# Seven products per pair in the second up projection too, its output split inside the down projection, and the weight sums moved

## The reference

```python
def swiglu(h, w_gate, w_up, w_down):
    return (jax.nn.silu(h @ w_gate) * (h @ w_up)) @ w_down
```

## Time and profile before

| | us |
|---|---|
| median of 3 runs (range) | 1692.26 (1689.1 to 1695.09) |
| the profiled execution: its own time, its span | 1692.44, 1690.6 |
| PE busy | 1623.7 (96% of the span) |
| DVE, ACT, POOL busy | 1115.1, 723.6, 344.0 |

### The profile page before, as it was taken

How to read it: one execution, slowest core, us unless ns; L and a number is a source line. 1 busy time by engine, 2 the same in 40 slices (tenths; PEclk the granted TensorE clock), 3 DMA queues, 4 the chain that set the end, 5 groups by cost and what they waited for, 6 DMA issues and landing times.

```text
span 1690.6 us, 23590 instructions
## 1 busy us (share of the span) xinstructions
PE 1623.7 (96%) x9069; PEld 1377.3 (81%) x9069; DVE 1115.1 (66%) x1793; ACT 723.6 (43%) x1158; POOL 344.0 (20%) x835
## 2 busy tenths in 40 slices
PE   6489999999999999999999999999989999999997
PEld 5378888888877877778888888888878899999886
DVE  6988666676664677646333336756746688888877
ACT  5465333332344767745222222234215544444554
POOL 2011877877861100000010110000010000000000
PEclk9789999999999999999999999999999999999999
DMA  8922344455477743455677774458973234555664
GB/s 346 383 86 92 110 151 148 136 181 173 138 163 154 157 125 131 119 137 152 218 183 213 195 196 138 129 171 217 261 207 114 86 118 157 153 158 157 194 190 140
DMA packets 169505, 282.26 MB, mean 167 GB/s; under 512 B 31489, under 2 KB 110705, under 8 KB 166066
## 3 DMA queue, kind: packets, MB, share of 16 engines
q1 hardware_dynamic: 137490, 218.36, 40.6%
q0 software_dynamic: 16992, 55.06, 14.5%
q10 hardware_dynamic: 14912, 7.34, 1.6%
HBM read 262.90 MB, written 70.77 MB: 197 GB/s over the span
## 4 chain that ended last, share of the span: by engine, by line
PE 86%; DVE 5%; DMA 4%; ACT 2%; issue 1%; SPq 1%; POOL 0%; DVEq 0%; ACTq 0%
PE bank L2207 26%; PE bank L2209 26%; PE bank L2208 26%; DVE ada L1419 1%; PE bank L2568 1%; PE bank L2541 1%; PE bank L2386 1%; DMA u_scratch<-us 1%; DVE htok L1403 1%; PE bank L2247 1%; PE bank L2697 1%; DMA raw<-in_fox_out 1%; ACT junk_h L914 1%; DMA raw<-in_fox_in 1%; DMA ada<-in_ada_w 1%
## 5 line engine op out<-in xcount | busy, mean ns | idle before, releaser
L2207 PE MATMUL bank<-hh,w_hi 128*128 128x512 f32 (+1 forms) x1440 | 520.8, 362 | 6.2 <-POOL hl L2202 3.9
L2208 PE MATMUL bank<-hl,w_hi 128*128 128x512 f32 (+1 forms) x1440 | 517.5, 359 | 0.0
L2209 PE MATMUL bank<-hh,w_lo 128*128 128x512 f32 (+1 forms) x1440 | 517.4, 359 | 0.0
L1316 DVE TENSOR_TENSOR w_lo<-raw,w_hi 128x1024 fp32r<-128x1024 f32 x320 | 373.5, 1180 | 196.6 <-ACT w_hi L846 191.5
L846 ACT ACTIVATE w_hi<-raw 128x1024 fp32r<-128x1024 f32 x320 | 325.4, 1021 | 378.1 <-DMA raw<-in_dn 114.7
L2207 PEld LDWEIGHTS bank<-hh,w_hi 128*128 128x128 f32 x1440 | 274.1, 190 | 48.3 <-POOL hl L2202 4.3
L2209 PEld LDWEIGHTS bank<-hh,w_lo 128*128 128x128 f32 x1440 | 274.0, 190 | 40.4
L2208 PEld LDWEIGHTS bank<-hl,w_hi 128*128 128x128 f32 x1440 | 274.0, 190 | 39.0
L2207 PE MATMUL bank<-w_hi,hid 128*128 128x512 f32 x352 | 138.1, 392 | 0.0
L2209 PE MATMUL bank<-w_hi,hid 128*128 128x512 f32 x352 | 137.1, 389 | 0.0
L2208 PE MATMUL bank<-w_lo,hid 128*128 128x512 f32 x352 | 137.0, 389 | 0.0
(11 more groups left out here) (354 smaller groups left out, 2595.0 us busy)
## 6 DMA issues: line engine op xcount, KB each, us to landing
raw<-in_up SPq DMA_DIRECT2D x94, 512.0 KB, 3.6
raw<-in_dn SPq DMA_DIRECT2D x55, 512.0 KB, 4.5
ada<-in_ada_w SPq DMA_DIRECT2D x24, 1024.0 KB, 8.5
v_scratch<-in_up POOLq DMA_DIRECT2D x25, 768.0 KB, 7.5
v_scratch<-in_dn POOLq DMA_DIRECT2D x24, 704.0 KB, 6.6
raw<-in_fox_in SPq DMA_DIRECT2D x32, 512.0 KB, 4.2
raw<-v_scratch SPq DMA_DIRECT2D x61, 256.0 KB, 2.7
raw<-in_up SPq DMA_DIRECT2D x57, 256.0 KB, 2.9
```

The lines of the kernel that those rows point to most:

```text
L1316: dve.tensor_tensor(w_lo[:, n % RING, 0:w], raw[:, n % RING, 0:w], w_hi[:, n % RING, 0:w].bitcast(F32), ALU.subtract).then_inc(lo_done, 1)
L2207: pe.matmul(dst, w_h, r_h, start=first, stop=False, skip_group_check=True)
L2208: pe.matmul(dst, w_h, r_l, start=False, stop=False, skip_group_check=True)
L2209: return pe.matmul(dst, w_l, r_h, start=False, stop=last, skip_group_check=True)
```

## The change

up2 now also does its pairs as seven products, for 18 of 22; `PLAIN2 = 4` stay plain. It needs 36 sums of its own. All sums are one chain now, in the order up2 (36), up3 (42), down3 (32): 16 between the turn tables, 34 over the 39 slots of fox, 28 in up2 from slot 4 on with one for each 2.5 slots, and the last 32 in up3, one for each 2 slots from slot 2 on. A slot of a pair counts like any other, and a pair has four of them now, not two.

up2's output goes unsplit to `hid_raw`. The combinations of `h` lie in the last tiles of `hid`, so only tiles 0 to 9 are split among the pairs, and tiles 10 to 21 in the first six slots of down2.

```diff
+UP2 = Stage("up2", 0, 1, 2, S_UP2, S_PAIRS2, PLAIN2, 0, 0, ((4, 7), (7, 10), (10, 13), (13, 16), (16, 19), (19, 22)))
+UP3 = Stage("up3", 1, 2, 4, S_UP3, S_PAIRS3, PLAIN3, UP2.paired, UP2.sums,
+            ((2, 5), (5, 8), (8, 11), (12, 15), (15, 18), (18, 20), (20, 22)))
+EARLY_HID = 10
...
+            def load_up(st):
+                src, i = dram[st.name], st.index
+                for n in range(2 * st.plain):
+                    load_fm(st.first + n, src[2 * st.tile(n // 2) + n % 2])
...
+                sp.wait_ge(sum_step, 16 * (st.sums_before + st.sums))
+                for p in range(st.paired):
+                    n, j = st.pairs + 4 * p, st.tile(st.plain + p)
+                    gate, val = src[2 * j], src[2 * j + 1]
+                    load_halves(n, gate[:, 0:T], v4[i][j])
+                    load_halves(n + 1, v2[i][j], gate[:, T:D])
+                    load_halves(n + 2, v1[i][j])
+                    load_halves(n + 3, val[:, T:D])
...
-            sp.wait_ge(sum_step, 16 * (UP_SUMS + 32))
-            for i, src in enumerate(sources):
+            for i, (src, sums) in enumerate(zip(sources, (0, 12, 24, 24, 32, 32, 32))):
+                sp.wait_ge(sum_step, 16 * (UP_SUMS + sums))
...
+            def split_hid_hi(j):
+                act.wait_ge(val_done, j + 1)
+                act.activation(hid[:, j, 0, :], hid_raw[:, j, 1, :], ACT.Copy).then_inc(hid_hi, 1)
...
+                    if st is UP2 and p < EARLY_HID:
+                        split_hid_hi(p)
...
+                    if q == 3 and EARLY_HID + 2 * idx < HT:
+                        if idx == 0:
+                            act.wait_ge(slot_mm, first)
+                        split_hid_hi(EARLY_HID + 2 * idx)
+                        split_hid_hi(EARLY_HID + 2 * idx + 1)
...
-            silu_up(S_UP2, 1, BANK_B[2])
+            silu_up_pairs(UP2)
...
+            def split_hid_lo(j):
+                dve.wait_ge(hid_hi, j + 1)
+                dve.tensor_tensor(hid[:, j, 1, :], hid_raw[:, j, 1, :], hid[:, j, 0, :].bitcast(F32), ALU.subtract)\
+                   .then_inc(hid_done, 1)
...
-            sums = up_sums()
+            sums = itertools.chain(up_sums(UP2), up_sums(UP3), down_sums())
             for k in range(PAIRS // 2):
                 turn_tables(k)
                 next(sums)
-            for t in range(UP_SUMS - PAIRS // 2):
-                pool.wait_ge(slot_mm, S_V + 1 + 3 * t // 2)
+            for t in range(34):
+                pool.wait_ge(slot_mm, S_V + 1 + 39 * t // 34)
                 next(sums)
-            assert next(sums, None) is None
-            weight_sums(S_UP2 + 2)
+            for t in range(UP_SUMS - 50):
+                pool.wait_ge(slot_mm, S_UP2 + 4 + 5 * t // 2)
+                next(sums)
             for i in range(KT):
                 pool.wait_ge(yh_done, i + 1)
                 pool.tensor_tensor(hl[:, i, :], yfm[:, i, :], hh[:, i, :].bitcast(F32), ALU.subtract).then_inc(y_done, 1)
+            for t in range(32):
+                pool.wait_ge(slot_mm, S_UP3 + 2 + 2 * t)
+                next(sums)
```

More of the change, by code:

```diff
@@ L8 @@
 from contextlib import ExitStack
+from dataclasses import dataclass
 import numpy as np
@@ L92, with paired, sums, end @@
 SPLIT_PAIR = HALF_DN // 2
+@dataclass(frozen=True)
+class Stage:
+    name: str
+    index: int
+    f: int
+    q: int
+    first: int
+    pairs: int
+    plain: int
+    before: int
+    sums_before: int
+    chunks: tuple
+    @property
+    def paired(self):
+        return HT - self.plain
+    @property
+    def sums(self):
+        return 6 * len(self.chunks)
+    @property
+    def end(self):
+        return self.pairs + 4 * self.paired
+    def tile(self, j):
+        return j // 2 + FH * (j % 2) if self.index else j
+UP2 = Stage("up2", 0, 1, 2, S_UP2, S_PAIRS2, PLAIN2, 0, 0, ((4, 7), (7, 10), (10, 13), (13, 16), (16, 19), (19, 22)))
+UP3 = Stage("up3", 1, 2, 4, S_UP3, S_PAIRS3, PLAIN3, UP2.paired, UP2.sums,
+            ((2, 5), (5, 8), (8, 11), (12, 15), (15, 18), (18, 20), (20, 22)))
+STAGES = (UP2, UP3)
+PAIRED = UP2.paired + UP3.paired
+Y_STEPS = 4 * PAIRED
+UP_SUMS = UP2.sums + UP3.sums
+EARLY_HID = 10
+def pair_slot(n):
+    for st in STAGES:
+        if st.pairs <= n < st.end:
+            return st, (n - st.pairs) // 4, (n - st.pairs) % 4
+    return None, 0, 0
 def landed_table():
@@ L101, in landed_table @@
                 parts = 2
-        if S_PAIRS <= n < S_DN3 and (n - S_PAIRS) % 4 in (0, 1):
+        st, _, place = pair_slot(n)
+        if st and place < 2:
             parts = 2
@@ L498, in build @@
         v3_made = sem("v3_made")
+        hid_hi = sem("hid_hi")
         pair_mm = sem("pair_mm")
@@ L1531, in make_v3, with silu_up_pairs @@
                    .then_inc(v3_made, 1)
-                dve.wait_ge(v3_made, p + 1)
-            def silu_up_pairs(first, f, base):
-                combinations = h_combinations()
-                for j in range(PLAIN):
-                    n = first + 2 * j
-                    if j == PLAIN - 1:
-                        make_v3(0)
+                dve.wait_ge(v3_made, st.before + p + 1)
+            def silu_up_pairs(st):
+                f, base = st.f, BANK_B[st.q]
+                combinations = h_combinations(st)
+                for j in range(st.plain):
+                    n = st.first + 2 * j
+                    if j == st.plain - 1:
+                        make_v3(st, 0)
                     lo(n + LEAD)
@@ L2319, in up, with up_pairs @@
                         bc(2, diag_gpost2, 4)
-            def up_pairs(q, f, first):
-                base = BANK_B[q]
-                first_slots(q, first, [bank[base], bank[base + 1]])
-                for i in range(2, 2 * PLAIN):
+            def up_pairs(st):
+                base, f, i_ = BANK_B[st.q], st.f, st.index
+                first_slots(st.q, st.first, [bank[base], bank[base + 1]])
+                for i in range(2, 2 * st.plain):
                     if i >= 4:
```

278 lines of the change are left out of this document (133 added, 145 removed).

## The result

The changed kernel takes 1760.03 us (median of 4 runs, 1741.8 to 1764.92), the kernel before beside it 1690.68 (4 runs, 1687.13 to 1695.09). The ratio is 1.0385 with a 95% interval of 1.0346 to 1.0423: 3.9% slower, above the upper end of the range on record, 1752. The changed kernel scatters more than the one before: 23 us between its four runs, for 8. The profiled execution took 1758.53 us, its span is 1756.8, so 66.2 us above the 1690.6 of before.

What follows compares the result with a forecast made beforehand. The prediction took PE, busy for 96% of the span, to bound the kernel. Its terms summed as 1692.4 - 14.4 + 18 + 19 + 2 - 1 = 1716.0 us, 1.4% slower, with a range of 1682 to 1752.

Steps and rivals of the forecast that it cites:

- the chain from the load to PE: In pairs, a late place 0 load holds `lo`, then `g_u2` behind it, then PE; only about 0.14 us are free.
- 1, products: In up2, a pair as seven products saves 0.80 us; 18 pairs give -14.4 us.
- 2, up2's pairs: In up2, sums delay the pairs' place 0 loads: 1.0 us per pair, +18 us, upper end +38.
- 3, up3's pairs: In up3, sums delay the pairs' place 0 loads: 1.0 us per pair, +19 us, upper end +29.
- 4, up2 to down2: At up2's end, `g_u2` stands behind down2's first load, landing in 5.4 us: +2 us (0 to 5).
- 5, fox: In fox, eight more sums, but more copies among them, one ahead of the load at 743.98: -1 us (-5 to +4).
- hidden split, down2: Splitting `hid` late in down2 costs nothing, as DVE and ACT have room and tile 10 is wanted five slots later.
- I take 1.0 us in both stages: Delay per pair chosen for up2 and up3, nearest the single-transfer prices 0.96 and 0.67; twice the delay gave 2.1 and 1.5.
- A sum's data are on the engines for only part of its 8 us: For up2's and up3's pairs, a reason given for pulling the delay per pair down, to 1.0 us.
- no wait of PE for `hid`: Sign expected in down2's profile after the change, with the split of `hid` priced at no cost.
- A: Rival: sums and place 0 loads fall apart in time, average delay under the free 0.14 us; 1679 us, chance 0.15.
- C: Rival: each place 0 transfer pays the full price, more if the clock drops; 1750 us, chance 0.15 for 1743 and above.

Runs made afterwards that it cites:

- e2: The changed kernel with the 28 sums in up2 and the 32 in up3 cut to 32 KB each, parts of the computation left out; 1679.43 us.
- e6: The changed kernel with the 12 late low splits of `hid` in down2 done by POOL, not DVE; 1762.19 us, ratio 1.0407.
- e10: The changed kernel with the 28 sums in up2 cut to a third of their bytes; 1735.03 us.
- e3: The changed kernel with the adding sums of up2 and up3 made plain copies of the same size; 1725.3 us.
- e1: The changed kernel with only the 28 sums in up2 cut to 32 KB each, those in up3 left whole; 1731.23 us.
- e4: The changed kernel with DVE's `lo(n + 4)` moved from ahead of `g_u2` to behind `g_val = z - g_u3` in each pair; 1718.79 us, ratio 1.0167.
- e9: e2 with DVE's late low splits in down2 behind each slot's table work, not ahead of it; 1679.8 us.
- e12: e2 with 10 of DVE's 12 late low splits in down2 cut to 16 columns; 1676.44 us.
- e13: e12 with ACT's high splits of the same 10 tiles cut to 16 columns as well; 1672.63 us.

## Why the prediction came out as it did

The direction and the chain from the load to PE were right, the size was not. Its terms, and what they measured:

| term | priced | measured | from |
|---|---|---|---|
| 1, products | -14.4 | -13.8 | up2, e2 less before |
| 2, up2's pairs | +18 | +47.0 (e6: +34.2) | up2, after less e2 |
| 3, up3's pairs | +19 | +32.2 | up3, after less e2 |
| 4, up2 to down2 | +2 | no wait seen | that load took 4.2 us, not 5.4 |
| 5, fox | -1 | -4.8 | start to up2 |
| hidden split, down2 | 0 | +6.4 | down2, after less before |

**Terms 2 and 3 were mis-sized.** The step that failed is "I take 1.0 us in both stages": a median excess of the landings less 0.14 us, as the price of every pair. The two prices, 2.6 us per pair (47.0 / 18) and 1.7 (32.2 / 19), lie even above the upper ends that the text gave, 2.1 and 1.5. The kept traces tell why. For each `v4` load, issue to landing is read one by one, and what it takes above 3.80 us (3.66 and the 0.14 that is free) is summed over the stage:

| stage of | `v4` loads over 5 us | sum above 3.80 | stage less e2's |
|---|---|---|---|
| up2, e2 | 0 of 18 | 0.4 | 0 |
| up2, e10 | 5 | 13.0 | 11.0 |
| up2, e3 | 7 | 19.4 | 20.5 |
| up2, e6 | 7 | 22.3 | 34.2 |
| up2, changed | 8 | 31.4 | 47.0 |
| up3, changed | 6 of 19 | 18.8 | 32.2 |
| up3, e3 | 11 | 25.6 | 24.9 |
| up3, e6 | 10 | 29.0 | 37.6 |
| up3, e10 | 11 | 36.8 | 45.4 |
| up3, e1 | 13 | 40.2 | 53.1 |

- *The median for the mean.* The median `v4` of the changed kernel's up2 takes 4.57 us, before in up3 3.54: 1 us later, as the prediction said it would be. At that median 18 pairs lose 14 us; load by load they lose 31.4, since 8 of the 18 take over 5 us. PE's waits in the stage are 25.2 + 5.8 = 31.0 us. A load issued just behind a sum lands with it (9.01 us at 845.86), one issued between two lands as ever.
- *The clock and the waits' edges had no price.* In up2 16.0 of the 47.0 us are no wait: PE is busy for 243.5 us with the matmuls that take it 227.5 in e2. The trace has the granted clock at its lower level for 34.1 us of the stage, and PE busy for 27.9 of these; with starts 0.21 us apart for 0.12 that loses 12 us, an estimate. The rest is in the waits' edges: the prediction's own pair lost 0.39 us, of which 0.12 are idle time (1507.87 to 1507.99). In e10's up2, at a clock of 1.00, ten waits come with 2.8 us of longer busy time, so 0.28 us each, and 15 waits make 4 us.
- *In up3 the loads of the other places.* The `v4` loads come to 18.8 us there, what term 3 says. But PE waits 24.9 us, 10.0 of them for `lo`, for which the sum had no term, and is busy for 7.1 us longer: an estimate of 1.5 us for 3.4 us at the lower clock, and some 6 for the edges of 21 waits.
- *A reason that pulled the wrong way.* "A sum's data are on the engines for only part of its 8 us" was used to bring the price down. The doses of e10 and e3 say otherwise: the stage paid for the time that a sum lasts.

So term 3's loads were sized right by luck: with the same sums they come to 18.8 us in one kernel and 40.2 in another.

By the Trainium skill (DMA: Bandwidth & Descriptors, Queues, rings and completion order) an engine drains a whole packet of descriptors of one queue before it turns to the next. The load that landed within a microsecond of its sum, after 9.01 us, agrees with such turns, and so do two others: the `v4` issued at 1023.31 (8.63 us, landed 0.5 us before the sum ahead of it) and, in the kernel before, the load issued at 743.98 (9.93 us, landed 0.5 us behind its sum). No run here shows how long a turn is, or rules out another cause in the queues.

**The chain through DVE was right.** The load's path (SP, ACT's `hi`, DVE's `lo(n + 4)`, `g_u2`, PE) is shown by e4: one line moved takes back 41 us. Its other half was not seen: with that line moved, PE waits for the slots themselves.

**"At no cost: the split of `hid`" failed.** The cover was counted by DVE's busy share (76.6 of 116.0 us) and by when tile 10 is wanted. But DVE's list in down2 has work with a date of its own, the tables and `ya`. The 12 splits, 7.7 us, push `ya` back until PE waits for it. The profile's row of the windows can't show that; the order of DVE's list can. The sign that the prediction named, no wait of PE for `hid`, came true and was the wrong one to watch.

**Term 5** lay at its bound, and the trace has it where the prediction looked. Before, the load that the chain shows at 743.98 took 9.93 us behind an adding sum, PE waited 3.5 us for the slot's `lo`, and from 744 to 775 the granted clock was 0.89. In the changed kernel, with a copy issued ahead, the same load took 6.83 us, PE's wait was 1.0 us and the clock 1.00. That the copy is the cause was not tested by itself.

**The rivals.** A's number, 1679, is what e2 gives (1679.43) when the sums are all but gone, but that is in part luck: fox gave -4.8 us for A's -1 and down2 +7.0, which A doesn't have, for its +2, and the two nearly cancel. Its mechanism, sums that hide, was false. C was the nearest, 1750, and had 0.15; it named the clock and the late loads of the other places.

What stays open: why the same sums meet the `v4` loads so differently from kernel to kernel (their phase against the pairs was not set by an experiment). The runs with parts left out, e1 to e3, e9, e10, e12 and e13, are one execution each.
